# A decoder layer in fp32: two FFN tiles at a time, half of the inner dimension by Strassen's seven products

## The reference

```python
x = x + y                                    # attention
h = rms_norm(x, norm_ffn[i])                 # 256 x 2048
x = x + (silu(h @ w_gate) * (h @ w_up)) @ w_down
gate = sigmoid(rms_norm(x, ple_norm[i]) @ ple_w_gate[i])
x = x + gate * (p[i] @ ple_w_proj[i])
```

## Time and profile before

| | before |
|---|---|
| median of 3 runs | 1203.43 us (1203.35 to 1203.49) |
| profiled execution | 1203.44 us, span 1201.7 us, granted clock 1.000 |
| busy PE / DVE / ACT / POOL | 1196.1 / 853.3 / 582.0 / 55.4 us |
| PE matmuls | 5364 |
| DMA | 238.5 MB, mean 198 GB/s |

### The profile page before, as it was taken

The page is one execution under the profiler, slowest core; times in us unless marked ns, Lnnn a source line. Parts: engine busy times, 40 slices in busy tenths (PEclk is TensorE's granted clock), DMA queues, the critical chain, the costliest instruction groups (busy, mean ns, idle before and its releaser), DMA issues.

```text
span 1201.7 us, 14639 instructions
## 1 busy us (share of the span) xinstructions
PE 1196.1 (100%) x5364; PEld 991.2 (82%) x5364; DVE 853.3 (71%) x1108; ACT 582.0 (48%) x719; POOL 55.4 (5%) x101
## 2 busy tenths in 40 slices
PE   9999999999999999999999999999999999999998
PEld 7888888888888888888888888888888888888887
DVE  5898989899667587686577677667666665656654
ACT  6556475665555544443444444444344444444442
POOL 0302021020001000000000000000000000000000
PEclk9999999999999999999999999999999999999999
DMA  7667576675568766666666666666565656565663
GB/s 263 211 197 213 172 227 193 199 227 178 172 212 261 232 204 177 208 192 183 202 193 182 188 207 194 184 202 196 182 205 182 207 180 207 180 207 177 223 213 108
DMA packets 133418, 238.50 MB, mean 198 GB/s; under 512 B 14658, under 2 KB 21876, under 8 KB 133364
## 3 DMA queue, kind: packets, MB, share of 16 engines
q1 hardware_dynamic: 133332, 237.82, 64.7%
q10 hardware_dynamic: 32, 0.01, 0.0%
HBM read 231.24 MB, written 6.55 MB: 198 GB/s over the span
## 4 chain that ended last, share of the span: by engine, by line
PE 93%; DVE 1%; issue 0%; DVEq 0%
PE acc L1253 91%; PE T L1300 1%; DVE squares L877 1%; DVE w_lo L812 0%; PE T L1328 0%; PE Z L1300 0%; PE acc L1447 0%; PE acc L1455 0%; PE Z L1310 0%; PE T L1310 0%; PE R L1318 0%; DVE x L1235 0%; DVE stage L1231 0%; DVE q_lo L1005 0%; DVE normed L870 0%
## 5 line engine op out<-in xcount | busy, mean ns | idle before, releaser
L533 ACT ACTIVATE w_hi<-raw 128x1024 fp32r<-128x1024 f32 x425 | 448.2, 1059 | 529.8 <-PE acc L1253 515.0
L812 DVE TENSOR_TENSOR w_lo<-raw,w_hi 128x1024 fp32r<-128x1024 f32 x425 | 516.7, 1223 | 258.7 <-ACT w_hi L533 255.7
L1253 PE MATMUL acc<-w_hi,xT_hi 128*128 128x512 f32 x1200 | 469.8, 392 | 0.4 <-DVE w_lo L812 0.3
L1253 PE MATMUL acc<-w_hi,xT_lo 128*128 128x512 f32 x1200 | 467.1, 389 | 0.0
L1253 PE MATMUL acc<-w_lo,xT_hi 128*128 128x512 f32 x1200 | 467.0, 389 | 0.0
L1253 PEld LDWEIGHTS acc<-w_hi,xT_hi 128*128 128x128 f32 x1200 | 225.3, 188 | 47.9 <-DVE w_lo L812 1.3
L1253 PEld LDWEIGHTS acc<-w_hi,xT_lo 128*128 128x128 f32 x1200 | 225.2, 188 | 47.5
L1253 PEld LDWEIGHTS acc<-w_lo,xT_hi 128*128 128x128 f32 x1200 | 225.4, 188 | 45.7
L1253 PE MATMUL acc<-w_hi,hT_hi 128*128 128x512 f32 x352 | 136.9, 389 | 0.0
L1253 PE MATMUL acc<-w_lo,hT_hi 128*128 128x512 f32 x352 | 136.9, 389 | 0.0
L1253 PE MATMUL acc<-w_hi,hT_lo 128*128 128x512 f32 x352 | 136.9, 389 | 0.0
(11 more groups left out here) (165 smaller groups left out, 628.7 us busy)
## 6 DMA issues: line engine op xcount, KB each, us to landing
raw<-in_sb_w_in SPq DMA_DIRECT2D x93, 512.0 KB, 4.5
raw<-in_ffn_w_gate SPq DMA_DIRECT2D x88, 512.0 KB, 3.7
raw<-in_ffn_w_up SPq DMA_DIRECT2D x88, 512.0 KB, 3.8
raw<-in_ffn_w_down SPq DMA_DIRECT2D x88, 512.0 KB, 4.4
raw<-in_sb_w_out SPq DMA_DIRECT2D x32, 512.0 KB, 4.0
raw<-in_ple_w_gate SPq DMA_DIRECT2D x32, 512.0 KB, 4.6
w_scratch<-w_blocks SPq DMA_DIRECT2D x12, 192.0 KB, 5.3
w_side<-w_scratch SPq DMA_DIRECT2D x48, 48.0 KB, 2.0
```

What stands on the lines that cost most here:

```text
L533: act.activation(w_parts[0][:, slot(u), 0:n, :], raw[:, slot(u), 0:n, :], ACT.Copy).then_inc(hi_ready, 1)
L812: dve.tensor_tensor(w_parts[1][:, slot(u), 0:n, :], raw[:, slot(u), 0:n, :], w_parts[0][:, slot(u), 0:n, :].bitcast(F32), ALU.subtract).th ...
L1253: last = pe.matmul(acc[pair][tb][:, :], parts[a][:, c, tb * P:(tb + 1) * P], w_parts[w][:, slot(u), i, :], start=(start and i == 0 and n = ...
```

## The change

Tiles 0, 1, 8, 9 and 10 stay as they are. Tiles 2 to 7 go in three pairs, and a pair in two "matrices" (gate, then up; six in all), each 16 row blocks by 1024 columns. A matrix is four steps of six units. In a step, two row blocks (2k and 2k+8) and the pair's two tiles form a 2x2 block matrix, as the two token blocks and the two row blocks do on the other side; Strassen's scheme in Winograd's form takes seven products P1 to P7 for them, in four units (two blocks each, the fourth with one). The two odd row blocks are multiplied as before, in two units of 12 matmuls, and are added in PSUM to the banks that become the results (P2, P3, P4, P8). All eight PSUM banks are used.

The sums of token blocks (S1 to S4) are made once, on DVE in tile 1 (`tokens`: eight instructions of 128x512, then one split of 128x2048). The differences of weight blocks (T1 to T4) are made by POOL, four of 128x512 for each step (`differences`). The seven products are put together by DVE out of PSUM, eight additions of 128x512 per matrix (`combine`), spread over the first four units of the next matrix; ACT keeps P1. Loads of a pair fetch one row block by 1024 columns. The finished tiles, all 11, are turned through HBM as x is.

```diff
-    D0 = C0 + FN * CU
+    PAIRS, KH, QUADS, MU = 3, KD // 2, 4, 24
+    MATRICES = 2 * PAIRS
+    AFTER_PAIRS = 2 + 2 * PAIRS
+    BEFORE_PAIRS, FS = 2, 5
+    C2 = C0 + BEFORE_PAIRS * CU
+    C8 = C2 + MATRICES * MU
...
+        P1, P2, P3, P4, P5, P6, P7, P8 = range(8)
+        banks = [Z[:, :], acc[0][0][:, :], acc[1][0][:, :], acc[0][1][:, :], R[:, :]]
+        banks += [t[:, :, :].rearrange("p a s -> p (a s)") for t in T] + [acc[1][1][:, :]]
...
+            def load_s(s):
+                sp.wait_ge(lo_ready, s_unit(s - 2, 3) + 1 if s >= 2 else C2 - 2 + 2 * s)
+                for i in range(2):
+                    sp.dma_start(raw[:, 2 * (s % 2) + i, :, :], pair_columns(s // QUADS, s % QUADS * 2 + KH * i)
+                                 ).then_inc(s_landed[s % 2], 16)
+            def load_n(n):
+                for i in range(2):
+                    if n == 0:
+                        sp.wait_ge(tokens_step, 8)
+                    else:
+                        sp.wait_ge(lo_ready, n_unit(n - 1, i) + 1)
+                    sp.dma_start(raw_n[:, i, :, :], pair_columns(n // QUADS, n % QUADS * 2 + 1 + KH * i)
...
+            load_s(1)
+            for s in range(SQ):
+                matrix, k = divmod(s, QUADS)
+                tile = matrix if matrix > 0 else 1
+                if matrix % 2 == 0 and k == 1:
+                    store_hidden(tile)
+                if s + 2 < SQ:
+                    load_s(s + 2)
+                if s + 1 < SQ:
+                    load_n(s + 1)
+                if matrix % 2 == 0 and k == 1:
+                    fetch_hidden(tile)
+                if matrix % 2 == 0 and matrix > 0 and k == 2:
+                    store_hidden(tile + 1)
+                if matrix % 2 == 0 and matrix > 0 and k == 3:
+                    fetch_hidden(tile + 1)
+            A = AFTER_PAIRS
...
+            def differences(s):
+                a, b = 2 * (s % 2), 2 * (s % 2) + 1
+                pool.wait_ge(s_landed[s % 2], 32 * (s // 2 + 1))
+                if s == 0:
+                    pool.wait_ge(tokens_ready, 1)
+                else:
+                    pool.wait_ge(lo_ready, s_unit(s - 1, 0) + 1)
+                pool.tensor_tensor(T13[:, 0, :], raw[:, a, 1, :], raw[:, a, 0, :], ALU.subtract).then_inc(differences_ready, 1)
+                pool.tensor_tensor(T13[:, 1, :], raw[:, b, 1, :], raw[:, a, 1, :], ALU.subtract).then_inc(differences_ready, 1)
+                if s > 0:
+                    pool.wait_ge(lo_ready, s_unit(s - 1, 2) + 1)
+                pool.wait_ge(differences_ready, 4 * s + 1)
+                pool.tensor_tensor(T24[:, 0, :], raw[:, b, 1, :], T13[:, 0, :], ALU.subtract).then_inc(differences_ready, 1)
+                pool.wait_ge(differences_ready, 4 * s + 3)
+                pool.tensor_tensor(T24[:, 1, :], raw[:, b, 0, :], T24[:, 0, :], ALU.subtract).then_inc(differences_ready, 1)
+            for s in range(SQ):
+                differences(s)
             norm(2, heads_end + NORM_STEPS)
...
+            def pair_hi(U, v, s):
+                k, i = divmod(v, 6)
+                act.wait_ge(unit_used, U - RING + 1)
+                if i < 4:
+                    a = 2 * (s % 2)
+                    if i == 0 or i == 2:
+                        act.wait_ge(differences_ready, 4 * s + 2 + i)
+                    else:
+                        act.wait_ge(s_landed[s % 2], 32 * (s // 2 + 1))
+                    source = (T13[:, :, :], raw[:, a:a + 2, 0, :], T24[:, :, :], raw[:, a + 1:a + 2, 1, :])[i]
+                else:
+                    act.wait_ge(n_landed[i - 4], 16 * (s + 1))
+                    source = raw_n[:, i - 4, :, :]
+                n = 1 if i == 3 else 2
+                act.activation(w_parts[0][:, slot(U), 0:n, :], source, ACT.Copy).then_inc(hi_ready, 1)
...
+            def block_hidden(j):
...
+                else:
+                    dve.wait_ge(x_stored, 16 * XN)
+                source = stage2 if BEFORE_PAIRS <= j < AFTER_PAIRS and j % 2 else stage
+                for tb in range(TB):
+                    dve.transpose(x_blocks[:, tb, :, :].rearrange("p b (c i) -> p b c i", i=Q),
+                                  source[:, tb, :].rearrange("p (c b j) -> p b c j", b=QN, j=Q)).then_inc(h_blocks_ready, 1)
...
+            def pair_lo(U, v, s):
+                i = v % 6
+                a = 2 * (s % 2)
+                source = (T13[:, :, :], raw[:, a:a + 2, 0, :], T24[:, :, :], raw[:, a + 1:a + 2, 1, :],
+                          raw_n[:, 0, :, :], raw_n[:, 1, :, :])[i]
+                n = 1 if i == 3 else 2
+                dve.wait_ge(hi_ready, U + 1)
+                dve.tensor_tensor(w_parts[1][:, slot(U), 0:n, :], source, w_parts[0][:, slot(U), 0:n, :].bitcast(F32),
+                                  ALU.subtract).then_inc(lo_ready, 1)
+            def combine(matrix, v):
+                U0 = C2 + matrix * MU
+                up = matrix % 2 == 1
+                now = 4 * (matrix // 2)
+                def add(to, a, bank, signal):
+                    dve.tensor_tensor(to, a, banks[bank], ALU.add).then_inc(signal, 1)
+                if v == 0:
+                    dve.wait_ge(product_read[P1], matrix + 1)
+                    dve.wait_ge(unit_used, U0 + 20 + 1)
+                    add(part_a, part_1, P6, product_read[P6])
+                    dve.wait_ge(product_read[P6], matrix + 1)
+                    add(part_b, part_a, P7, product_read[P7])
+                if v == 1:
+                    dve.wait_ge(product_read[P7], matrix + 1)
+                    add(junk[:, :] if up else stage2[:, 1, :], part_b, P5, product_read[P5])
+                    add(part_a, part_a, P5, product_read[P5])
+                if v == 2:
+                    dve.wait_ge(unit_used, U0 + MU)
+                    add(part_1 if up else stage[:, 0, :], part_1, P2, product_read[P2])
+                    add(part_b if up else stage[:, 1, :], part_b, P4, product_read[P4])
+                if v == 3:
+                    dve.wait_ge(product_read[P5], 2 * matrix + 2)
+                    add(part_a if up else stage2[:, 0, :], part_a, P3, product_read[P3])
+                    to = junk[:, :] if up else stage2[:, 1, :]
+                    add(to, to, P8, product_read[P8])
+                if up and v in (4, 5):
+                    dve.wait_ge(pair_gated, now + 4)
+                    for i in (2 * v - 8, 2 * v - 7):
+                        dve.wait_ge(product_read[(P2, P4, P3, P8)[i]], matrix + 1)
+                        part = (stage, stage2)[i // 2][:, i % 2, :]
+                        dve.tensor_tensor(part, part, (part_1, part_b, part_a, junk[:, :])[i],
+                                          ALU.mult).then_inc(pair_multiplied, 1)
+            def pair_gate(matrix, i):
+                part = (stage, stage2)[i // 2][:, i % 2, :]
+                dve.wait_ge(pair_sig_ready, 4 * (matrix // 2) + i + 1)
+                dve.scalar_tensor_tensor(out=part, in0=part, scalar=rstd2[:, i % 2:i % 2 + 1], in1=junk[:, :],
+                                         op0=ALU.mult, op1=ALU.mult).then_inc(pair_gated, 1)
+            def pair_matrix(matrix):
+                for v in range(MU):
+                    pair_lo(C2 + matrix * MU + v, v, matrix * QUADS + v // 6)
+                    if matrix > 0:
+                        combine(matrix - 1, v)
+                    if matrix == 0 and v == 2:
+                        times_up(1, C2 - 1)
+                        p_lo()
+                    if matrix % 2 == 0:
+                        tile = matrix if matrix > 0 else 1
+                        if v == 6:
+                            block_hidden(tile)
+                        if v == 18:
+                            hidden_lo(tile)
+                        if matrix > 0 and v == 13:
+                            block_hidden(tile + 1)
+                    else:
+                        if matrix > 1 and v == 6:
+                            hidden_lo(matrix)
+                        if v in (7, 9, 11, 13):
+                            pair_gate(matrix, (v - 7) // 2)
...
+                    if j == A:
...
             def gate_up(j, first=False):
...
                     part, k = C_HEAD[u] if first else divmod(u, DU)
                     if first and part == 0:
                         pe.wait_ge(x_side_lo_ready, D_UNITS[k][-1] // CB + 1)
-                    products(C0 + j * CU + u, u, xT, D_UNITS[k], part, k == 0, k == DU - 1, (C_P0, C_P1)[part] + j)
+                    if j == AFTER_PAIRS and k == 0:
+                        for bank in ((P2, P4), (P3, P8))[part]:
+                            pe.wait_ge(product_read[bank], MATRICES)
+                    products(U0 + u, u, xT, D_UNITS[k], part, k == 0, k == DU - 1, (C_P0, C_P1)[part] + s)
...
+            def seven_products(matrix, k):
+                low = [a[:, 2 * k, :] for a in xT]
+                high = [a[:, 2 * k + KH, :] for a in xT]
```

(55 more changed lines are left out.)

253 lines of the change are left out of this document (208 added, 45 removed).

## The result

| | before | after |
|---|---|---|
| median of all runs | 1203.41 us | 1232.38 us (1231.90 to 1234.07) |
| ratio | | 1.0241, 95% interval 1.0230 to 1.0253 |
| profiled execution | 1203.44, span 1201.7 | 1234.07, span 1232.3 |
| PE matmuls | 5364 | 5292 |

The change costs 2.4%, 29 us, although PE has 72 matmuls fewer. The page of after, answering: busy time, then the shares of the last chain by engine and by line.

A forecast was written before the change was run, and what follows sets the result against it. PE bounds the kernel before; in the changed pairs DVE, held up by POOL's reads, becomes the bound. Pairs +13.3, exit +1.6, entry +0.5 make +15.4 on the 1203.4 us: 1219 us, range 1187 to 1243.

The forecast's parts named there:

- PE's gain: In the pairs, 72 fewer matmuls save 16.4 us; PE alone would need 245.6 us in place of 262.0.
- The old turn, SP and ACT: Old transposes gone; the turn through HBM and SP's queue cost nothing; ACT's 29 of 40.9 us a matrix is hidden.
- DVE's bill: DVE's splits, additions and other work over the six matrices, without holds: 202.7 us.
- The hold: In the pairs, a POOL difference meeting a DVE instruction with two SBUF inputs holds DVE up 1.1 us.
- The middle I took: Hold per POOL difference set at 1.1 us, between estimates of 0.99 and 1.24.
- Cover: Of 92 differences within the pairs, 26 run beside DVE work they do not hold up; 66 hold DVE.
- the rival of no cover: All 92 differences in the pairs hold DVE up: 1247 us, or 1260 at 1.24 each; chance 0.12.
- The pairs: DVE bounds the pairs at 275.3 us, 13.3 us longer than the 262.0 before.
- 0.5 at the entry: At the pairs' entry, first load, differences, ACT and DVE against PE's 6 units, 16.4 us: costs 0.5 us.
- The exit: First plain tile after the pairs waits for two additions that begin only after the last product: 1.6 us, no cover.
- The rival "only POOL waits": In the pairs, DVE's reads are never held up, or the hold is 0.55 us: 1189 us, up to 1194; chance 0.24.
- The 0.03 us of the earlier trace: Before's split at 105.60, just after a POOL start, took 1.25 us, not 1.22: taken as a trace of POOL holding DVE.

The follow-up runs named there:

- experiment 1: Changed kernel with POOL writing a constant (memset) in place of the four weight differences, same waits and signals: 1197.85 us, ratio 0.9951 to before.
- experiment 3: Kernel of before, no Strassen, all 11 plain tiles turned through HBM: 1203.69 us, ratio 1.0001.
- experiment 6: Changed kernel with POOL making only the 20 of 96 differences that run beside DVE's additions out of PSUM, DVE the others: 1205.54 us, ratio 1.0016.
- experiment 7: As the kernel with 20 differences on POOL beside PSUM additions, but POOL's share made one step later, without that cover: 1228.50 us, ratio 1.0209.
- experiment 2: Changed kernel with each POOL difference replaced by an instruction with one input of 512 columns: 1199.09 us, ratio 0.9958.
- experiment 4: Changed kernel with all differences made on DVE, POOL idle: 1215.64 us, ratio 1.0096.
- experiment 5: Changed kernel with the gate of the first plain tile after the pairs summed in P6's and P7's banks, free earlier: 1227.59 us, ratio 1.0202.

## Why the prediction was right, and what it sized wrongly

The sign, the mechanism and the range held; 1219 was 13 us low.

*PE's gain.* 72 matmuls at 0.2274 us. Right: without POOL's reads the pairs take 249.2 us (experiment 1), 3.6 above the 245.6.

*The old turn, SP and ACT.* Costed at nothing; experiment 3 gives nothing, and 62.6 us of DVE against the 60 expected.

*DVE's bill.* 202.7 forecast, 207.8 measured without reads.

*The hold.* 1.1 forecast, 1.10 measured (2.31 - 1.21), and seen on both engines. The time of a difference alone, 1.29 us, was above both of my figures (1.1 and 1.24): the hold is less than the instruction. Its parts were also wrong: one input holds 0.42, two hold 1.10, so reading both costs more than twice one. The middle I took hit the sum of two errors: that the forecast had 1.1 was luck. The estimate for the whole instruction from the figure of the Trainium skill (GPSIMD Engine Reference, section 3.1) was 1.12, under the 1.29 here. The Trainium skill's rule of the shared port (SBUF — State Buffer, section Who interferes with whom) sets a VectorE instruction with two SBUF inputs against a GpSimd one that reads SBUF, and not against one that only writes. It holds here: no hold with memset, none beside additions that read PSUM, 1.10 us beside splits. The prediction had cited the exclusion as for the whole length; the measured hold is 1.10 of the 1.29 us.

*Cover.* 26 differences free, 66 holding: 66 x 1.1 = 72.6 us forecast, 63 measured (270.75 - 207.79). Set beside experiment 1 instruction by instruction, 62 of DVE's are longer by 0.4 us or more: by matrix 10, 12, 10, 12, 10 and 8. The forecast's 66 holds are 14, 12, 10, 12, 10 and 8, so the count of cover was right in every matrix but the first. So the rival of no cover is out for this kernel, and experiments 6 and 7 show that it would have been real: the same 20 differences cost nothing or 23 us, by place.

*The pairs.* By matrix, forecast (bill plus holds) and measured starts to starts:

| matrix | 0 | 1 | 2 | 3 | 4 | 5 | sum |
|---|---|---|---|---|---|---|---|
| forecast | 44.8 | 46.1 | 47.2 | 47.2 | 47.2 | 42.8 | 275.3 |
| measured | 50.4 | 46.2 | 47.3 | 48.2 | 47.4 | 46.2 | 285.7 |

Four matrices are within 1.1 us. Of the 10.4 us too few, 9.0 are in the first and the last: I let DVE's work fill them, and there it could not. In matrix 5 only three steps have differences; the fourth took PE's 10.2 us, not DVE's bill of 6.3. In matrix 0 the term "0.5 at the entry" failed. I had weighed the first load against PE's 6 units, but not the state in which DVE enters: it began the first split at 466.58, 2.4 us ahead of PE, and POOL's second set of differences followed the first at once and held up the next splits.

```profile
470.14 2.14 DVE L1405 TENSOR_TENSOR w_lo<-T,w_hi 128x1024 fp32r<-128x1024 f32 x1
...
475.82 0.50 PE L1783 MATMUL acc<-w_hi,tokens_hi 128*128 128x512 f32 x1 [1.81 <-DVE w_lo L1405]
478.04 0.80 PE L1783 MATMUL acc<-w_hi,xT_hi 128*128 128x512 f32 x1 [1.26 <-DVE w_lo L1405]
478.64 0.63 PE L1783 MATMUL acc<-w_lo,xT_hi 128*128 128x512 f32 x1
```

PE waited three times, and then ran 12 matmuls at the lower clock, 2.4 us. Without the reads matrix 0 takes 41.1 us: the entry's loss is the port's too.

*The exit.* 1.6 us forecast, 3.6 measured and 2.5 of low clock behind it. I let the two additions begin when the last product ended, at 754.67. Ahead of them in DVE's program stand the plain tile's first three splits and the additions of P6, P7 and P5's pair, and these could not start earlier. DVE ran them without a pause from 750.93:

```profile
749.84 1.06 ACT L691 ACTIVATE w_hi<-raw 128x1024 fp32r<-128x1024 f32 x1 [0.90 <-DMA raw<-in_ffn_w_gate]
...
750.93 1.22 DVE L1033 TENSOR_TENSOR w_lo<-raw,w_hi 128x1024 fp32r<-128x1024 f32 x1 [1.23 <-ACT w_hi L691]
...
755.13 0.68 DVE L1415 TENSOR_TENSOR spare<-spare,R 128x512 f32<-128x512 f32 x1
755.73 1.22 DVE L1033 TENSOR_TENSOR w_lo<-raw,w_hi 128x1024 fp32r<-128x1024 f32 x1
756.86 0.68 DVE L1415 TENSOR_TENSOR p_sb<-p_sb,acc 128x512 f32<-128x512 f32 x1
```

DVE was not late here: it had just been idle for 1.23 us, behind ACT, and ACT had waited for the plain tile's first load. SP issued that load at 746.05, as soon as the split that started at 745.33 had left its slot. The gap is the same where DVE has room. In experiment 1 it is 3.5 us, and 3.5 to 3.7 in experiments 2, 4, 6 and 7. Experiment 1's first product of the plain tile:

```profile
722.59 0.47 PE L1610 MATMUL acc<-w_hi,xT_hi 128*128 128x512 f32 x1 [3.35 <-DVE p_sb L1415]
```

So the exit's cost is one of order and of the late first load, not of POOL's reads. No run moved that load.

*The clock.* No term of the sum had it. At the entry and the exit a wait made by another engine was paid twice, once as idle PE and once as slow matmuls; inside matrices that DVE bounds, the slow matmuls of experiment 5 cost nothing.

*The rival "only POOL waits"* had 0.24 and is refuted by the 2.31 us splits. The 0.03 us of the earlier trace rows was the right sign of it. The 3.91 us wait of POOL in the earlier trace rows was not the pattern: after's longest difference is 2.37 us, one split and its own read. What passed POOL over there stays open.

## What to carry to other kernels

Before work is moved to POOL to relieve DVE, add POOL's reads to DVE's bill as a hold for each instruction that would meet a DVE instruction with two SBUF inputs; here the hold (1.10 us) was dearer than the work on DVE itself (0.60). POOL's reads are free beside DVE instructions that read PSUM or one SBUF operand, so they should be placed there by hand. Once an engine is forecast to be the bound of a stretch, cost the entry of that stretch, and every chain through a shared buffer, with that engine late. At the exit, write down all that stands ahead of the awaited instruction in its engine's program, and when the next stretch's first load may start.

## What the runs showed of the hardware

- A DVE subtraction of 128x1024 with both inputs in SBUF: 1.21 us alone, 1.63 when POOL reads one operand of 512 columns, 2.31 when it reads two, 1.21 to 1.23 when POOL only writes.
- POOL's own times for 128x512: memset 0.53, one input 0.62, two inputs 1.29 us with the port free.
- DVE's block transposes (two of 128x512, 1.29 us) and its additions out of PSUM (0.68 us) kept their lengths beside a difference, and the difference kept its 1.29 to 1.30.
- In the profiles of the nine kernels with pairs, PE's granted clock fell to 1.2 GHz around the pairs after each of the six gaps of 3.5 to 3.7 us. It fell after waits of 2.0 to 3.1 us in some cases (after 2.03 us twice in experiment 5 and once in experiment 7) and not in others (2.0 us at 629 and 725 us in after, 2.03 at 721 us in experiment 7), and after no single wait of 1.7 us or less. It stayed down for some 6 to 12 matmuls, 0.427 us apart.
